# Encoder layer for two sequences: embedding product ahead of the feed-forward part, gate input split early and loaded row by row

## The chip, the cores and the metric

One core of one Trainium2 chip. The metric is the device time of one execution in microseconds (us); lower is better.

## What is computed

One encoder layer with shared weights is applied to two sequences of 1,024 tokens and 1,024 channels, all in float32:

```
x = x + RMSNorm(concat(pool mixer, attention) @ w_out)
x = x + RMSNorm(SwiGLU(RMSNorm(x)))                    D_FF = 2816
e = p @ w_ple_proj                                     p: 1024 x 256
g = sigmoid(x @ w_ple_gate + b_ple_gate)
return x + e * g
```

The change concerns the last three lines. Below, x after the feed-forward residual is called x2, e the embedding product, x2 @ w_ple_gate the gate product.

## The kernel before

The program has three parts.

**Mixer** (0 to 1,008 us). For each sequence: projections, attention, output projection. It leaves the residual x1 in DRAM (`x1_turned`, channels on partitions) and the feed-forward input in `h2_forms`.

**Feed-forward** (1,008 to 2,315 us). The products use a seven-product scheme for 2x2 blocks. `UNITS` lists the work: for each sequence 11 gate/up units, then 8 down units; each unit has 7 steps (`product`, L1158 to L1176). Every float32 operand is held as two float32r halves, a rounded `hi` and the rest `lo`, and every product is three matmuls (hi*hi, hi*lo, lo*hi). ACT rounds (`hi`), DVE subtracts (`lo`). The moving operand lives in `reg`, 7 forms of up to 4 k-tiles; weights pass through `wraw`, `ws` (sums made by POOL) and `ring` (3 slots, one per step). PE, ACT, DVE, POOL and SP each run their own list in program order and meet only at semaphores. SP issues the transfers of the part. During the gate units of sequence 1 the kernel finishes sequence 0: `norm_in` (SP), `norm_step` (ACT, DVE) and an addition on POOL form x2 of sequence 0 row by row (a row is one k-tile, 128 channels x 1,024 tokens, 512 KB) through the three slots of `stg`, and store it in `x2_turned` as plain float32.

**Embedding and gate** (2,315 us to the end). `x2r` holds both halves of the 8 rows of x2 and lies in the memory of `reg`. So the rows of sequence 0 are loaded into `stg` after the last step of the feed-forward part and split there by ACT and DVE. There are 16 tiles m of 128 output channels, 8 for each sequence. PE does per tile: `gate_tile` (48 matmuls of 512 columns), `turn_y` of the tile before (8 transposes), `embed_tile` (12 matmuls). ACT takes the sigmoid, DVE multiplies by e straight out of PSUM and adds x2 (`y_sum`, L2058 to L2070), PE transposes, ACT copies to `yrow`, SP stores. x2 of sequence 1 is made beside the tiles of sequence 0: its 4 MB of f are loaded at once into `fb`, squared in tiles 2 and 3, summed over the channels by PE in the middle of tile 5 (`token_sums`), scaled by DVE in tiles 5 and 6 (L2112), added to x1 by POOL (L928), and split in tile 7. The tokens p are transposed by PE before the first tile of each sequence (`turn_tokens`), and a weight tile of w_ple_proj comes with each tile.

Its tile loop on PE:

```
for m in range(2 * KT):
    gate_tile(m)
    if m % KT == 0:
        turn_tokens(m // KT)
    if m:
        turn_y(m - 1)
    embed_tile(m)
turn_y(2 * KT - 1)
```

## Time and profile before

| | us |
|---|---|
| median of 3 runs (lowest to highest) | 2611.19 (2607.82 to 2617.57) |
| the profiled execution, its device time | 2615.33 |
| its span in the profile | 2613.1 |
| PE busy in the span | 2403.5 (92%) |
| DVE busy | 1678.6 (64%) |
| ACT busy | 1091.4 (42%) |
| POOL busy | 899.3 (34%) |
| DMA engines, mean share of q1 | 42.4% |

PE is TensorE's matmul row, DVE VectorE, ACT ScalarE, POOL GpSimd, SP the queue that issues transfers. The clock column of a stretch is the share of full speed that TensorE was granted: 1.00 is 2.4 GHz, 0.50 is 1.2 GHz. A busy share over the whole span mixes stages; the table by stage in the first group of rows below is what says where PE waits.

### The profile page before, as it was taken

The numbers are of one execution on the slowest core, as the hardware profiler recorded it, in microseconds if no ns is written. First come the engines' busy times: TensorE is split into PE (matmuls) and PEld (weight loads), VectorE is DVE, ScalarE is ACT, GpSimd is POOL, SyncE is SP. The second block draws the span as 40 slices with busy tenths as digits, with TensorE's granted clock in tenths as the row PEclk, the third lists the DMA queues.
The fourth block names the chain that finished last, engine by engine and source line by source line (L and its number), as shares of the span: only waits on it lengthen the run. The fifth ranks groups of instructions, "written<-read, shape, count | busy, mean of one in ns | idle before, by whom it ended". The sixth has DMA issues, their size and how long they took to land.

```text
span 2613.1 us, 32818 instructions
## 1 busy us (share of the span) xinstructions
PE 2403.5 (92%) x11528; PEld 1992.0 (76%) x11528; DVE 1678.6 (64%) x1814; ACT 1091.4 (42%) x1607; POOL 899.3 (34%) x549
## 2 busy tenths in 40 slices
PE   7989999398999992999999999899999999969898
PEld 6878878387788771888888888678788888857677
DVE  6678854266888442777677555788888855554632
ACT  4368854332888442433333322344433332223322
POOL 0024520200445013454444354544455535520300
PEclk9989999699999995999999999999999999989999
DMA  4000022610000346444454876745557687554422
GB/s 140 17 25 25 2 107 81 192 41 14 20 17 1 139 128 207 152 157 153 135 171 164 335 265 215 224 158 199 168 181 249 234 332 267 197 217 150 126 80 71
DMA packets 299889, 376.26 MB, mean 144 GB/s; under 512 B 16464, under 2 KB 213968, under 8 KB 299600
## 3 DMA queue, kind: packets, MB, share of 16 engines
q1 hardware_dynamic: 299152, 372.08, 42.4%
q0 software_dynamic: 576, 2.10, 0.3%
q8 instruction: 93, 1.52, 0.2%
q14 instruction: 68, 0.56, 0.1%
HBM read 249.35 MB, written 124.78 MB: 143 GB/s over the span
## 4 chain that ended last, share of the span: by engine, by line
PE 63%; issue 16%; POOL 8%; DMA 5%; DVE 4%; SPq 2%; ACT 1%; POOLq 1%; DVEq 0%; ACTq 0%
PE ps L1175 42%; PE ps L934 18%; PE ps L937 3%; DMA stg<-h_forms 1%; SPq L506 1%; DMA h_forms<-forms 1%; POOL win_s L785 1%; DMA xb<-x_turned 1%; POOL win_s L793 1%; DVE reg L1859 1%; POOL win_s L794 1%; DVE ring L1850 1%; POOL win_s L780 1%; POOL heads L806 1%; POOL wout_a L829 1%
## 5 line engine op out<-in xcount | busy, mean ns | idle before, releaser
L1175 PE MATMUL ps<-reg,ring 128*128 128x512 f32 x5544 | 1267.2, 391 | 66.7 <-DVEq L1863 47.1
L1175 PEld LDWEIGHTS ps<-reg,ring 128*128 128x128 f32 x5544 | 1044.8, 189 | 288.7 <-issue 47.4
L1271 ACT ACTIVATE ring<-wraw 128x1024 fp32r<-128x1024 f32 (+2 forms) x152 | 143.7, 946 | 413.5 <-PE ps L1175 376.4
L1850 DVE TENSOR_TENSOR ring<-wraw,ring 128x1024 fp32r<-128x1024 f32 (+2 forms) x152 | 228.7, 1505 | 96.5 <-ACT ring L1271 95.7
L934 PE MATMUL ps<-win,ht 128*128 128x512 f32 (+1 forms) x1152 | 234.3, 362 | 40.4 <-DVE win L1706 40.3
L934 PEld LDWEIGHTS ps<-win,ht 128*128 128x128 f32 x1152 | 191.7, 193 | 71.5 <-DVE win L1706 42.8
L934 PE MATMUL ps<-x2r,gsp 128*128 128x512 f32 x768 | 184.6, 400 | 26.6 <-DVE x2r L2076 19.4
L1271 ACT ACTIVATE ring<-ws 128x1024 fp32r<-128x1024 f32 (+2 forms) x114 | 107.9, 947 | 237.8 <-PE ps L1175 226.0
L1790 DVE TENSOR_TENSOR pt<-ps,pt 128x512 fp32r<-128x512 f32 x256 | 172.4, 687 | 48.9 <-ACT pt L1271 46.4
L1850 DVE TENSOR_TENSOR ring<-ws,ring 128x1024 fp32r<-128x1024 f32 (+2 forms) x114 | 175.9, 1543 | 42.5 <-ACT ring L1271 41.4
L934 PEld LDWEIGHTS ps<-x2r,gsp 128*128 128x128 f32 x768 | 148.0, 194 | 60.8 <-issue 16.7
L1271 ACT ACTIVATE pt<-ps 128x512 fp32r<-128x512 f32 x256 | 153.1, 605 | 60.3 <-PE ps L937 56.7
L1760 DVE TENSOR_REDUCE negmax<-ps 128x1 f32<-128x1024 f32 x128 | 155.8, 1217 | 15.1 <-PE ps L934 15.1
L937 PEld LDWEIGHTS ps<-ident,prob 128*128 128x128 f32 x1024 | 126.3, 142 | 46.1 <-DVE pt L1790 15.4
L937 PE MATMUL ps<-ident,prob 128*128 128x128 f32 x1024 | 156.1, 276 | 4.2 <-DVE pt L1790 4.1
L934 PE MATMUL ps<-keys,qs 128*128 128x512 f32 x512 | 154.8, 426 | 1.7 <-ACT prob L1364 1.7
L868 POOL TENSOR_TENSOR ws<-wraw,ws 128x1024 f32<-128x1024 f32 (+2 forms) x38 | 80.1, 2109 | 210.6 <-DMA wraw<-in_w_up 133.2
L934 PE MATMUL ps<-pt,values 128*128 128x512 f32 x512 | 149.4, 415 | 0.0
L1364 ACT ACTIVATE prob<-ps,negmax 128x1024 f32<-128x1024 f32 x128 | 143.2, 1119 | 3.1 <-DVE negmax L1760 3.1
L899 POOL TENSOR_TENSOR acc<-acc,ev 128x1024 f32<-128x1024 f32 x36 | 105.9, 2943 | 103.3 <-DVE ev L1871 103.3
L874 POOL TENSOR_TENSOR ws<-wraw,ws 128x1024 f32<-128x1024 f32 (+2 forms) x38 | 102.5, 2699 | 64.4 <-DVE ring L1850 64.4
L862 POOL TENSOR_TENSOR ws<-wraw 128x1024 f32<-128x1024 f32 (+2 forms) x38 | 101.0, 2658 | 64.1 <-DVE ring L1850 49.6
(199 smaller groups left out, 3064.2 us busy)
## 6 DMA issues: line engine op xcount, KB each, us to landing
reg<-ff_forms SPq DMA_DIRECT2D x42, 1536.0 KB, 10.1
ff_forms<-fhi SPq DMA_DIRECT2D x88, 512.0 KB, 3.2
wraw<-in_w_gate SPq DMA_DIRECT2D x88, 256.0 KB, 4.2
wraw<-in_w_up SPq DMA_DIRECT2D x88, 256.0 KB, 4.6
ff_forms<-ev SPq DMA_DIRECT2D x44, 512.0 KB, 2.9
wraw<-in_w_down SPq DMA_DIRECT2D x48, 384.0 KB, 5.9
stg<-h_forms SPq DMA_DIRECT2D x28, 512.0 KB, 5.6
reg<-ff_forms SPq DMA_DIRECT2D x14, 1024.0 KB, 5.0
```

What stands on the lines that cost most here:

```text
L862: ins = nc.gpsimd.tensor_tensor(s0, raw_block(u, 0, 0), raw_block(u, 1, 0), ALU.subtract)
L868: ins = nc.gpsimd.tensor_tensor(s1, raw_block(u, 1, 1), s0, ALU.subtract)
L874: ins = nc.gpsimd.tensor_tensor(s1, raw_block(u, 0, 1), s1, ALU.subtract)
L899: nc.gpsimd.tensor_tensor(t, t, ev[:, 0], ALU.add).then_inc(S["acc_sum"], 1)
L934: return nc.tensor.matmul(out, lhs, rhs, start=start, stop=stop)
L937: return nc.tensor.transpose(out, src, ident[:])
L1175: last = nc.tensor.matmul(ps[:, 2 * chain + m, :], ring[:, st % 3, a, m, k * P:(k + 1) * P], reg[:, k, i, e, :], start=OPENS[i] and k == 0 ...
L1271: copy = lambda out, src, **k: nc.scalar.activation(out, src, ACT.Copy, **k)
L1364: nc.scalar.activation(prob[:, s % 2, :], pair(2 * (s % 2)), ACT.Exp, bias=negmax[:, s:s + 1], scale=1.0, accum_out=rowsum[:, s:s + 1]).th ...
L1760: V.tensor_reduce(negmax[:, s:s + 1], pair(2 * (s % 2)), AX.X, ALU.max, negate=True)\
L1790: V.tensor_tensor(pt[at][:, 1], ps[:, 4 + half, :].rearrange("p (k n) -> p k n", k=4), f(pt[at][:, 0]), ALU.subtract).then_inc(S["p_split" ...
L1850: V.tensor_tensor(ring_block(u, st, 1), weight_source(u, i), f(ring_block(u, st, 0)), ALU.subtract).then_inc(S["w_split"], 1)
```

## The change

- **Embedding product first.** Before the first feed-forward step SP loads p of both sequences (2 MB) and w_ple_proj (1 MB); PE transposes p (32 transposes) and makes all 16 tiles of e (192 matmuls). ACT copies each tile out of PSUM to `eo`, SP stores it to `e_turned`. The loads of the first weights and of `reg` come behind the loads of p. `y_sum` gets e back from DRAM into `er`.
- **x2 of sequence 0 split early.** Its making starts at step 33 of sequence 1's gate units, one row every 5 steps (`row_at`, five phases), all in fixed slots of `stg`: 0 the row, 1 first x1 and then the `lo` half, 2 the `hi` half. ACT makes `hi`, DVE `lo`; SP stores both to `x2_split` beside the plain row.
- **By rows.** In the last unit each finished step frees one form of `reg`, and SP loads a split row of x2 (1 MB) into it (`x2_in`). PE then runs tiles 0 and 1 together, row by row, with the two halves of each row already there.
- **Own rows for each sequence.** The rows of sequence 1 get memory of their own (other halves of the forms, and `ring`). f of sequence 1 comes through four slots of one row each: squares in tiles 0 and 1, token sums right after tile 2, the scaling, addition and splitting two rows per tile in tiles 4 to 7. Each of these rows is loaded, and stored back for `y_sum`, in its turn.
- `reg` is laid out form by form; loads into it have one piece per partition where they had several. Weights of the gate have three split slots and are asked for three tiles ahead.

```diff
+SQ_AT, SPLIT_AT, TOKENS_AT, ROOT_AT, INV_AT, ROW_AT, ROW_STEPS = 7, (24, 26), (25, 27), 28, 29, 33, 5
+def norm_at(u, i):
+    return NP * u.j + i if u.seq == 1 and not u.down else -1
+def row_at(u, i, phase):
+    n, r = divmod(norm_at(u, i) - ROW_AT - phase, ROW_STEPS)
+    return n if r == 0 and 0 <= n < KT else None
...
+    x2s_d = nc.dram_tensor("x2_split", (P, KT, 2, 2, CH), F32, kind="Internal").ap()
+    e_d = nc.dram_tensor("e_turned", (NSEQ, P, KT, SEQ), F32, kind="Internal").ap()
...
-        reg = sb(s_reg, "reg", [P, KG, NP, 2, CH], F32R)
-        sb(s_reg, "reg_rest", [P, 2 * CH])
+        reg = sb(s_reg, "reg", [P, NP, KG, 2, CH], F32R)
         s_reg.close()
         s_acc = ExitStack()
-        sb(s_acc, "reg_front", [P, 3 * NP * 2 * CH])
-        acc = sb(s_acc, "acc", [P, 8, 2, CH])
...
+        def x2_row(s, k):
+            if s == 0:
+                return reg[:, k, 0:2] if k < NP else reg[:, 1, 2:4]
+            return reg[:, (0, 2, 3, 4, 5, 6)[k], 2:4] if k < 6 else ring[:, k - 6]
...
+                n = row_at(u, i, 0)
+                if n is not None:
+                    if n:
+                        sp.wait_ge(S["x2_out"], 16 * n)
+                        sp.wait_ge(*at_least("x2s_out", 32 * n))
+                    else:
+                        sp.wait_ge(S["stg_free"], PIECES)
+                    sp.dma_start(stg[:, 0], f_d[0, :, n, :]).then_inc(S["stg_in0"], 16)
+                    sp.dma_start(stg[:, 1].rearrange("p (c n) -> p c n", c=2),
+                                 x1t_d[0:2, :, n, :].rearrange("c p n -> p c n")).then_inc(S["stg_in1"], 16)
+                n = row_at(u, i, 3)
+                if n is not None:
+                    sp.wait_ge(S["x2_sum"], n + 1)
+                    sp.dma_start(x2_d[0, :, n, :], stg[:, 0]).then_inc(S["x2_out"], 16)
+                n = row_at(u, i, 4)
+                if n is not None:
+                    sp.wait_ge(S["x2_hi"], n + 1)
+                    sp.dma_start(x2s_d[:, n, :, 0, :], stg[:, 2].rearrange("p (t n) -> p t n", t=2))\
+                        .then_inc(on("x2s_out"), 16)
+                    sp.wait_ge(S["x2_split"], n + 1)
+                    sp.dma_start(x2s_d[:, n, :, 1, :], stg[:, 1].rearrange("p (t n) -> p t n", t=2))\
+                        .then_inc(on("x2s_out"), 16)
+            def gate_in(m):
...
+            def x2_in(k):
+                if k == KT - 1:
+                    sp.wait_ge(S["a_end"], NU - 1)
+                    sp.wait_ge(S["step_done"], NP * (NU - 2))
+                    sp.wait_ge(*at_least("x2s_out", 32 * KT))
+                else:
+                    sp.wait_ge(S["step_done"], NP * (NU - 1) + k + 1)
+                dst = x2_row(0, k).rearrange("p t e n -> p (t e n)").bitcast(F32)
+                sem = on("x2_row") if k == KT - 1 else on(f"op_in{k}")
+                sp.dma_start(dst, x2s_d[:, k].rearrange("p t e n -> p (t e n)")).then_inc(sem, 16)
...
+            sp.dma_start(pwraw[:], w_proj.rearrange("(k p) n -> p k n", p=P)).then_inc(S["p_in"], 16)
+            for s in range(NSEQ):
+                sp.dma_start(ptok[:, s], p[s * NT:(s + 1) * NT].rearrange("t p n -> p t n")).then_inc(S["p_in"], 16)
             for m in range(2):
                 weights_in(UNITS[0], m)
-            for i in range(2):
+            fill_in(0, 0)
+            weights_in(UNITS[1], 0)
+            for i in range(1, 5):
                 fill_in(0, i)
-            weights_in(UNITS[1], 0)
-            for i in range(2, NP):
+                for m in range(4 * i - 4, 4 * i):
+                    e_store(m)
+            for i in range(5, NP):
                 fill_in(0, i)
             for u in UNITS:
                 for i in range(NP):
@@ -662,8 +758,13 @@
...
+                    if u.n == NU - 2 and i == 5:
+                        gate_in(0)
+                        gate_in(1)
+                    if u.n == NU - 1:
+                        x2_in(i - 1 if i else KT - 1)
...
+            def row_in(n):
+                a = 2 * (n % 2)
                 if n >= 2:
-                    sp.wait_ge(S["y_ready"], n - 1)
-                sp.dma_start(xr[:, n % 2], x2_d[0, :, n, :]).then_inc(S[f"xr_in{n % 2}"], 16)
-            def tokens_in(s):
-                if s:
-                    sp.wait_ge(S["pp_turned"], 1)
-                sp.dma_start(ptok[:], p[s * NT:(s + 1) * NT].rearrange("t p n -> p t n")).then_inc(S["p_in"], 16)
-            def x1_in(n):
-                if n >= 2:
-                    sp.wait_ge(S["fx_done"], n - 1)
-                sp.dma_start(xb[:, n % 2].rearrange("p (c n) -> p c n", c=2),
-                             x1t_d[2:4, :, n, :].rearrange("c p n -> p c n")).then_inc(S[f"xb_in{n % 2}"], 16)
+                    sp.wait_ge(*at_least(f"cs_out{n % 2}", 16 * (n // 2)))
...
+                if m + 3 < 2 * KT:
+                    gate_in(m + 3)
+                if m == 0:
+                    for n in range(4, KT):
+                        square_in(n)
+                if m == 2:
+                    row_in(0)
+                    row_in(1)
+                if m and m + 1 < 2 * KT:
+                    e_in(m + 1)
+                    residual_in(m + 1)
+                if 4 <= m < KT:
+                    for n in (2 * (m - 4), 2 * (m - 4) + 1):
+                        row_out(n)
+                        if n + 2 < KT:
+                            row_in(n + 2)
                 if m:
-                    if 2 <= m + 1 < KT:
-                        residual_in(m + 1)
...
+            turn_embed(0)
+            turn_embed(1)
+            for m in range(2 * KT):
+                embed_tile(m)
+            pe.wait_ge(*at_least("e_done", 2 * KT))
...
+                if last:
+                    done.then_inc(S["gate_done"], 1)
...
+            pe.wait_ge(S["g_split"], 2)
+            for j, k in enumerate(ROWS0):
+                if k == KT - 1:
+                    pe.wait_ge(*at_least("x2_row", 16))
+                else:
+                    pe.wait_ge(*at_least(f"op_in{k}", 16 * (2 * len(DPART) + 1)))
+                for m in range(2):
+                    gate_row(m, k, j == 0, j == KT - 1)
+            turn_y(0)
+            for m in range(2, 2 * KT):
+                pe.wait_ge(S["g_split"], m + 1)
+                pe.wait_ge(S["sig_done"], m - 1)
+                for k in range(KT):
+                    if m == KT:
+                        pe.wait_ge(S["x2_split"], KT + k + 1)
+                    gate_row(m, k, k == 0, k == KT - 1)
+                if m == 2:
+                    for t in range(2):
+                        pe.wait_ge(S["sum_split"], 3 + t)
+                        token_sums(t, sumhl, 4 + t)
+                turn_y(m - 1)
             turn_y(2 * KT - 1)
...
+                if -4 <= st < 0:
+                    for m in range(4 * st + 16, 4 * st + 20):
+                        e_tile(m)
+                if inside and u.n == NU - 1 and i in (2, 4):
...
+                    act.wait_ge(S["sum_done"], 4)
+                    root(rnorm[:], pair(4), D).then_inc(S["sum_root"], 1)
...
             def y_sum(m):
-                s, n = divmod(m, KT)
                 t = sig[:, m % 2]
                 dve.wait_ge(S["sig_done"], m + 1)
-                dve.wait_ge(S["proj_done"], m + 1)
-                V.tensor_tensor(t, t, pair(4), ALU.mult).then_inc(S["prod_done"], 1)
+                dve.wait_ge(*at_least(f"er_in{m % 2}", 16 * (m // 2 + 1)))
+                V.tensor_tensor(t, t, er[:, m % 2], ALU.mult).then_inc(S["prod_done"], 1)
                 dve.wait_ge(S["prod_done"], m + 1)
-                if s == 0:
-                    dve.wait_ge(S[f"xr_in{n % 2}"], 16 * (n // 2 + 1))
-                else:
-                    dve.wait_ge(S["fx_done"], n + 1)
-                V.tensor_tensor(t, t, xr[:, n % 2] if s == 0 else fb[:, n], ALU.add).then_inc(S["y_ready"], 1)
-            tile_lo(0)
-            for k in range(KT):
-                use = PLE_USE + k
-                dve.wait_ge(S["x2_hi"], k + 1)
-                V.tensor_tensor(x2r[:, k, 1], stg[:, use % 3, :], f(x2r[:, k, 0]), ALU.subtract)\
-                    .then_inc(S["x2_split"], 1)
...
+                    if m == 1:
+                        dve.wait_ge(S["sq_done0"], KT)
+                        for t in range(2):
+                            dve.wait_ge(S["sum_done"], 2 + t)
+                            sum_halves(t, sumhl)
+                if m in (2, 3):
                     dve.wait_ge(S["sum_root"], 2)
-                    go(V.reciprocal(rnorm[:], rnorm[:]))
-                if m in (5, 6):
-                    for k in range(4 * (m - 5), 4 * (m - 5) + 4):
-                        V.scalar_tensor_tensor(out=fb[:, k], in0=fb[:, k], scalar=gpost2[:, k:k + 1], in1=rnorm[:],
+                    part = rnorm[:, (m - 2) * CH:(m - 1) * CH]
+                    go(V.reciprocal(part, part))
+                if 4 <= m < KT:
+                    for k in (2 * (m - 4), 2 * (m - 4) + 1):
+                        a = 2 * (k % 2)
+                        t = chain_slot(a)
+                        dve.wait_ge(*at_least(f"cs_in{a}", 16 * (2 + k // 2 + 1)))
+                        V.scalar_tensor_tensor(out=t, in0=t, scalar=gpost2[:, k:k + 1],
+                                               in1=rnorm[:].rearrange("p (t n) -> p t n", t=2),
                                                op0=ALU.mult, op1=ALU.mult).then_inc(S["x2_scaled"], 1)
-            y_sum(2 * KT - 1)
+                    for k in (2 * (m - 4), 2 * (m - 4) + 1):
+                        dve.wait_ge(S["x2_hi"], KT + k + 1)
```

PE at the start of the feed-forward part, before. The names: `hrow` and `h` are the last transposes of the mixer, L1175 is `product`.

```order
L937 MATMUL ps<-ident,hrow 128x128 x8
L937 MATMUL ps<-ident,h 128x128 x8
L227 ISA
L952 REGISTER_ALU
L952 COMPARE_AND_BRANCH
L1175 MATMUL ps<-reg,ring 128x512 x3516
```

PE at the same place now (L1294 is `product`):

```order
L1056 MATMUL ps<-ident,hrow 128x128 x8
L1056 MATMUL ps<-ident,h 128x128 x8
L246 ISA
L1071 REGISTER_ALU
L1071 COMPARE_AND_BRANCH
L1056 MATMUL ps<-ident,ptok 128x128 x32
L1053 MATMUL ps<-pturn,psp 128x512 x192
L1294 MATMUL ps<-reg,ring 128x512 x3372
```

The 32 transposes of p and the 192 embedding matmuls stand between the mixer and the first step.

SP in iteration 5 of its tile loop now. `wraw` receives the gate weights of tile 8, `er` and `xr` the embedding and residual rows of tile 6; `x2_turned<-ev` stores a finished row of x2 of sequence 1, and `ev`, `cs3` receive the f and x1 of the row two further on; `y` is the output of tile 4; the last row is the weight tile of iteration 6.

```order
L696 DMA wraw<-in_w_pgate 128x8x128
L788 DMA er<-e_turned 128x1024
L797 DMA xr<-x2_turned 128x1024
L826 DMA x2_turned<-ev 128x1024
L818 DMA ev<-f_turned 128x1024
L820 DMA ev<-x1_turned 128x2x512
L826 DMA x2_turned<-ev 128x1024
L818 DMA ev<-f_turned 128x1024
L820 DMA cs3<-x1_turned 128x2x512
L833 DMA y<-yrow 128x8x128
L696 DMA wraw<-in_w_pgate 128x8x128
```

Each load of f waits until the store of the row before it in the same slot has landed; the weight tile of the next iteration stands behind them all. Before, this loop held no store of x2.

## Rows read from the trace of the kernel before

**Rows 1.** Stages: length, busy time (and instructions) of PE, PEld, DVE, ACT, POOL; clock, DMA share, GB/s.

```profile
1000.00:1038.00 38.00, 7.82 (x24) 5.96 (x24) 12.96 (x8) 9.29 (x9) 7.38 (x4) 0.59 0.78 238
...
2302.00:2345.00 43.00, 24.44 (x95) 18.89 (x94) 20.24 (x18) 10.03 (x11) 7.95 (x3) 0.80 0.61 208
...
2440.00:2500.00 60.00, 43.94 (x193) 35.25 (x192) 40.63 (x28) 19.25 (x22) 23.23 (x8) 0.87 0.41 121
```

**Rows 2.** Timeline of PE at the start of the feed-forward part: start, length, work [idle before].

```profile
1026.09 7.82 PE L1175 MATMUL ps<-reg,ring 128*128 128x512 f32 x24 [47.07 <-DVEq L1863]
1038.26 22.10 PE L1175 MATMUL ps<-reg,ring 128*128 128x512 f32 x84 [4.35 <-DVE ring L1850]
```

**Rows 3.** The first transfer that SP issues for the feed-forward part.

```profile
1008.52 0.39 SPq L542 DMA_DIRECT2D wraw<-in_w_gate  x1
```

**Rows 4.** Two narrow stretches, columns as in group 1.

```profile
1012.00:1024.00 12.00, 0.00 (x0) 0.00 (x0) 5.49 (x2) 4.23 (x4) 7.00 (x3) 0.50 0.81 254
...
2100.00:2120.00 20.00, 20.00 (x90) 16.56 (x89) 15.39 (x13) 9.10 (x12) 11.03 (x6) 1.00 1.04 401
```

**Rows 5.** Timeline of PE from the last feed-forward steps to the end.

```profile
2289.98 24.77 PE L1175 MATMUL ps<-reg,ring 128*128 128x512 f32 x108 [0.24 <-DVE ring L1850]
2329.27 6.78 PE L934 MATMUL ps<-x2r,gsp 128*128 128x512 f32 x18 [14.52 <-DVE x2r L2076]
...
2387.37 1.03 PE L937 MATMUL ps<-ident,sig 128*128 128x128 f32 x8
2388.16 2.98 PE L934 MATMUL ps<-pturn,psp 128*128 128x512 f32 x12
2390.98 11.05 PE L934 MATMUL ps<-x2r,gsp 128*128 128x512 f32 x48
...
2600.62 1.03 PE L937 MATMUL ps<-ident,sig 128*128 128x128 f32 x8
...
2607.03 1.51 PE L937 MATMUL ps<-ident,sig 128*128 128x128 f32 x8 [2.64 <-DVE sig L2070]
```

**Rows 6.** Groups after 2,316 us: line, work, count | busy us, mean ns | idle before.

```profile
L928 POOL TENSOR_TENSOR fb<-fb,xb 128x1024 f32<-128x1024 f32 x8 | 24.9, 3120 | 140.4 <-DVE fb L2112 138.2 <-DMA xb<-x_turned 2.1
L2048 DVE TENSOR_TENSOR gsp<-graw,gsp 128x1024 fp32r<-128x1024 f32 x16 | 19.6, 1224 | 55.7 <-ACT psp L1271 55.5
L2064 DVE TENSOR_TENSOR sig<-sig,ps 128x1024 f32<-128x1024 f32 x16 | 19.5, 1218 | 75.7 <-PE ps L934 75.7
L1626 ACT ACTIVATE sig<-ps,bgate 128x1024 f32<-128x1024 f32 x16 | 17.8, 1113 | 65.7 <-PE ps L934 65.7
...
L1271 ACT ACTIVATE gsp<-graw 128x1024 fp32r<-128x1024 f32 x16 | 16.9, 1056 | 116.1 <-DMA praw<-in_w_proj 116.1
...
L2070 DVE TENSOR_TENSOR sig<-sig,xr 128x1024 f32<-128x1024 f32 x8 | 12.0, 1504 | 0.3
```

**Rows 7.** Transfers after 2,316 us: count, KB each, median us from issue to landing.

```profile
graw<-in_w_pgate SPq DMA_DIRECT2D x16, 512.0 KB, 5.2
y<-yrow SPq DMA_DIRECT2D x16, 512.0 KB, 3.6
```

**Rows 8.** Transfers from 1,880 to 2,300 us, columns as in group 7.

```profile
stg<-f_turned SPq DMA_DIRECT2D x8, 512.0 KB, 5.7
...
x_turned<-stg SPq DMA_DIRECT2D x8, 512.0 KB, 4.3
```

**Rows 9.** Timeline of DVE in gate unit 6 of sequence 1.

```profile
1914.42 1.22 DVE L1938 TENSOR_TENSOR ev<-ev,ps 128x1024 f32<-128x1024 f32 x1 [2.46 <-PE ps L1175]
...
1926.59 1.28 DVE L2003 SCALAR_TENSOR_TENSOR stg<-stg,gpost,rnorm 128x1024 f32<-128x1024 f32 x1 [0.38 <-DMA stg<-f_turned]
...
1928.92 2.62 DVE L1850 TENSOR_TENSOR ring<-wraw,ring 128x1024 fp32r<-128x1024 f32 x1
...
1938.71 3.42 DVE L2003 SCALAR_TENSOR_TENSOR stg<-stg,gpost,rnorm 128x1024 f32<-128x1024 f32 x1
```

**Rows 10.** Timeline of SP's transfers in the same unit.

```profile
1930.29 0.68 SPq L542 DMA_DIRECT2D wraw<-in_w_up  x1
```

537 lines of the change are left out of this document (277 added, 260 removed).

## Prediction, made before the changed kernel had been run

> **What bounds the kernel now.** I read the table by stage first [rows 1]. Over the feed-forward part PE is busy all the time; only three places leave it idle, and they are where a change of order can act: the start of the feed-forward part (7.8 us busy of 38), the start of the gate part (24.4 of 43), and the turn from sequence 0 to sequence 1 (43.9 of 60). Then the timeline of PE at each place. At the first, step 0 runs at 1026.1 after 47 us without work, and steps follow one another without a gap from step 1 on, at 1038.3 [rows 2]; SP asked for the first data at 1008.5 [rows 3] and the DMA engines were 81% busy behind it [rows 4]. At the second, the last step ends at 2314.75 and the first gate matmul starts 14.5 us later; its first 18 take 6.8 us where 48 take 11.05 once it runs steadily [rows 5], and the stretch has a granted clock of 0.80 [rows 1]. From 2314.75 to the end of the span are 298.35 us. That is the tail that the change rebuilds.
>
> **The tail, without new waits.** A tile now costs PE 10.9 us for the gate, 0.8 for the transposes, 2.8 for the embedding (starts 2387.37, 2388.16, 2390.98 [rows 5]). The change leaves 11.7. Tiles 0 and 1 by rows take 2 x 10.9 = 21.8. At the end, transposing the last tile starts at 2607.03 and the span ends 6.1 later; before it stand the sigmoid (1.1), product and sum (1.2 each), with 0.3 for the handing over [rows 6], 3.8 in all, now that no embedding stands there. With the first gate matmul 2.5 us after the last step (an eviction of 1.2 and the landing of the store that it waits for, now behind x2 rows) the tail would be 2.5 + 21.8 + 14 x 11.7 + 0.8 (a last transposing beside the tiles) + 1.1 (token sums) + 3.8 + 6.1 = 200. Will the x2 rows be there? The last unit has seven steps of 12 matmuls, 2.7 us each, so their loads begin at about -19; 8.4 MB until 20 us after the last step want 215 GB/s; 401 GB/s stands in a stretch with large pieces [rows 4]. At that rate a row of 1 MB takes 2.7 us, as long as PE takes for it in two tiles. So I cost the rows at nothing, with the last unit's own matmuls as the cover; if that cover went, PE would wait for the last row, which is asked for only after the last step.
>
> **The tail's new waits.** Three, in order of time after the last step (0).
> 1. PE transposes tile 0 right behind tiles 0 and 1, with nothing between. The gates end at 24.4, tile 0 is summed at 26.8: 2.4 us.
> 2. The token sums are now wanted after tile 2, which ends at 38.5. DVE sums tile 0, splits a weight tile, adds four squares (to 32.4); then SP may load the last of the next four, and only behind it the gate weights of tile 4. These land 5.2 later [rows 7], at 38.1; ACT rounds them (1.06) ahead of its four squares (to 43.4), DVE adds and halves (to 46), PE sums, waits for the second halves, sums (48.3). PE's transposing ends at 49.3 where 40.4 was possible: 9 us, and about 1.6 for a clock that has dropped. The latter is from the 18 matmuls of 6.8 us, which at full clock take 4.1 [rows 5].
> 3. The rows of sequence 1. In tiles 4 to 7 one iteration is a ring of waits over four engines and SP, since the gate weights of the next iteration are asked for behind two stores that must land: DVE scales row a (1.3 [rows 9]), POOL adds x1 (3.1 [rows 6]), SP stores and waits (3.6 [rows 7]), issues two loads (0.9), stores row b and waits (3.6), two loads, the output, the weight tile (1.7 for issuing), which lands after 5.2, ACT rounds (1.06), DVE subtracts (1.22), and only then scales again. That is 21.7, taken as 22, where a tile takes PE 11.7. The first scaling is possible at 78.6 (tile 4 ends at 73.5; sigmoid, sum, weight split 5.1), the fourth at 144.6; row 7 is then split and multiplied after 1.3 + 2 x 3.1 + 1.1 + 1.2 + 1.4, plus 1.4 at a low clock, 12.6. Tile 8 ends at 157, where 120 was possible: 37 us, the largest new wait.
> The seven tiles that follow and the end bring the tail to 157.2 + 1.0 + 7 x 10.9 + 6 x 0.8 + 1.6 + 3.8 + 6.1 = 250.8. Against 298.35 it gives back **47.5 us**.
>
> **The start.** 3.1 MB of p and w_ple_proj stand ahead of the weights. At 280 GB/s, between 254 with small pieces and 401 [rows 4], they are there at about 1,020.5. 32 transposes at half clock (8 take about 1 us at full clock [rows 5], so 16 take 4), rounding and splitting of two tiles (2.1 and 2.4 [rows 6]) let PE begin at 1,029. Sixteen tiles at 2.8 are 45; an eviction (1.1) and 2 us of gaps between ACT's other copies follow: step 0 at 1,077, step 1 at 1,083. Before, step 1 was at 1038.3. **Plus 45.** The embedding was 45 us in the tail, so almost nothing of it is hidden in the gap of 47 us: that gap ends when the memory is free and the data has come, and p has to come first. The price from below is 42 (data at 401 GB/s, no gaps). From above: 22 MB in all (p, weights, `reg`, 8.4 MB of e stored) at 254 GB/s are 87 us, which puts step 1 at 1,096, plus 58. I stay near the lower end, since e is stored in pieces of 4 KB.
>
> **The feed-forward part.** PE is fed by DVE. In gate unit 6 a step's weights are split at 1931.5 and wanted four steps (24 matmuls, 5.45 us at the gate's pace) after 1914.4, at 1936.2 [rows 9]: 4.7 us to spare. Eight more rounding copies on ACT (1.06) and eight subtractions on DVE (1.2) fit. What costs is the order. A row that is due in step 1 is loaded by SP only after the unit's weights, at 1931.0 on the scale of this unit [rows 10]. It lands 5.7 later [rows 8], and DVE, which wants it at 1931.5, holds back the split for the next step; 5.7 less what is spared leaves 1 to 2 us. Of eight rows two stand so. Stores have to land (4.3 [rows 8]) before the next load, at one row per five steps that fits. One us for the two weight splits in the last unit. **Plus 4**, with 0 and 12 as bounds. The layout of `reg` is at nothing: the part's loads were hidden already.
>
> **Sum.** +45 + 4 - 47.5 = +1.5 us on the profiled execution of 2615.33: **2617 us**. That execution is 4.1 above the median of the three, 2611.19, and 2617 is 0.2% above the median. A measurement of this kernel can tell 0.5%, 13 us, from no change.
>
> **Two rules of the Trainium skill.** Scaling takes 1.28 us alone and 3.42 with POOL at work [rows 9]; the product with e read PSUM and took 1.22, the addition of two SBUF rows 1.50 on average [rows 6]. The Trainium skill, SBUF — State Buffer, "Who interferes with whom", says why: a DVE instruction with two SBUF inputs and a GpSimd instruction that reads SBUF exclude each other. It speaks against taking e from SBUF. By that rule the trace agrees, and the product can be held up to one POOL addition; in item 3 it stands beside the ring, so the sum stays. The Trainium skill, DMA: Bandwidth & Descriptors, "Anatomy of one DMA", fits 2.0 us plus size over 436 GB/s, 3.2 us for 512 KB; the weight tile at 5.2 stands against it. An estimate of the ring by that page is 18.9 us, and the sum 9 us lower.
>
> **Rivals.**
> - *A, faster: the ring does not bind.* If SP's waits overlap more than I think (stores landing in under 3 us, weights that come beside them), the rows of sequence 1 stay behind tiles of 11.7 us and the 37 us of item 3 go. For it: after 2,500 the DMA engines of before are lightly loaded, and the ring has no large piece of work. Against: five landings in a row. 2617 - 37 = 2580. Chance 0.20.
> - *B, slower: the start is bound by stores.* ACT may evict a tile only when the store of two tiles earlier has landed, and SP stands between stores waiting for `reg` pieces. With 1.1 + 4.3 + 0.5 us per two tiles PE's 5.6 decides; it turns when a landing takes over 4.5 us, and at the upper bound above it adds 13: 2630. Chance 0.16.
> - *C, slower: DVE starves the ring of weights.* If the loads of x2 rows land over 10 us after issue (split rows, f, x1 and the feed-forward forms in one queue), each of eight rows holds DVE for more than it has to spare, about 5 us: 2617 + 40 = 2657. For it: DVE waits in program order for ACT, ACT for POOL, POOL for DVE. Against: before, the same kind of load gave one wait of 0.38 [rows 9]. Chance 0.12.
> - *Forecast* 0.52, with its own range from 2600 (start 42, ring 20) to 2638 (start 52, ring 25, part 8).
>
> **Numbers.** Faster by over 0.5% is under 2598: A and 0.06 of the forecast, 0.26. Slower is over 2624: B, C less a little, and 0.09 of the forecast, 0.34. Same 0.40. The range takes in A and the forecast and leaves out half of A and most of C: 2580 to 2640.
>
> **What would show it.** Step 1 near 1,083 and 192 embedding matmuls behind one another before it. The first gate matmul within 3 us of the last step. An idle of 7 to 9 us ahead of the token sums. In tile 8 two waits of PE for the split of rows, together over 30 us, and between the scalings of DVE 22 us. I would be wrong if tile 8 starts and ends like its neighbours, if step 1 is past 1,090, or if PE shows waits for `ring` of several us at each row of sequence 0.

## The result, and where the time went

| | before | after |
|---|---|---|
| median (lowest to highest), us | 2613.22 (2607.82 to 2617.57), 4 runs | 2675.84 (2673.46 to 2676.88), 4 runs |
| the profiled execution, device time | 2615.33 | 2676.23 |
| its span | 2613.1 | 2674.4 |

The ratio is 1.0239, with a 95% interval from 1.0217 to 1.0261: the change makes the kernel 2.4% slower. The prediction was 2617 us with a range from 2580 to 2640, and is wrong: neither the time nor the range holds.

The ledger is made from the two traces. For the feed-forward part I compare the moment at which DVE makes the same addition (the one in step 2 of each unit, 38 in all, counted from 0) with the trace of before:

| unit | what the change put ahead of it | later than before, us |
|---|---|---|
| 1 to 21 | the embedding product | 43.8 (42.9 to 43.6 in units 19 to 21) |
| 24 | squares and token sums of sequence 0 | 59.5 |
| 31 | rows of x2 of sequence 0 | 85.0 |
| 37 | loads of x2 rows, gate weights | 86.8 |
| end of the last step | | 2401.92 - 2314.75 = 87.2 |

Unit 24 already holds most of the first row of x2. Counted from unit 23 (57.0) the squares and sums have 13.2 and the rows 28.0, where the table gives 15.7 and 25.5.

From the end of the last step to the end of the span are 2674.4 - 2401.92 = 272.5 us, 25.9 less than the 298.35 of before. The three sections: +43.8 (predicted +45), +43.4 (predicted +4), -25.9 (predicted -47.5); together +61.3, the difference of the spans.

**The start.** Timeline of PE after, against [rows 2] (columns: start, length, work, idle before and its releaser):

```profile
1018.75 6.53 PE L1056 MATMUL ps<-ident,ptok 128*128 128x128 f32 x32 [41.27 <-DMA ptok<-in_p]
1026.84 11.33 PE L1053 MATMUL ps<-pturn,psp 128*128 128x512 f32 x48 [1.56 <-DVE pturn L2162]
1039.80 22.01 PE L1053 MATMUL ps<-pturn,psp 128*128 128x512 f32 x96 [1.62 <-ACT eo L1396]
1062.52 11.16 PE L1053 MATMUL ps<-pturn,psp 128*128 128x512 f32 x48 [0.71 <-ACT eo L1396]
1076.51 33.75 PE L1294 MATMUL ps<-reg,ring 128*128 128x512 f32 x135 [2.82 <-ACT eo L1396]
```

Step 0 is at 1076.5 where 1,077 was predicted, and 192 matmuls stand ahead of it. Small gaps end with ACT's eviction into `eo`; they looked harmless, and runs 5, 10 and 11 show what stands behind them.

**The feed-forward part.** Before, the timeline of PE shows one unbroken piece of work there (1800 matmuls):

```profile
1881.44 408.29 PE L1175 MATMUL ps<-reg,ring 128*128 128x512 f32 x1800 [0.87 <-ACT rnorm L1275]
```

After, the waits from 1,900 to 2,240 us are (engine and line, waited for; total us, times, longest):

```profile
DVE stg L2144 <- DMA stg<-f_turned: 25.8, 5, 8.9
...
PE ps L1294 <- DVE ring L1993: 19.6, 7, 6.2
...
ACT stg L1396 <- POOL stg L1041: 17.1, 6, 9.4
```

L2144 is DVE's scaling of an x2 row, L1993 its split of feed-forward weights. The timeline of DVE shows how the first wait becomes the second: the scaling waits 6.1 us for its load, and two splits of weights that PE needs stand behind it in program order.

```profile
1992.37 1.22 DVE L1993 TENSOR_TENSOR ring<-wraw,ring 128x1024 fp32r<-128x1024 f32 x1
1999.66 1.28 DVE L2144 SCALAR_TENSOR_TENSOR stg<-stg,gpost,rnorm 128x1024 f32<-128x1024 f32 x1 [6.08 <-DMA stg<-f_turned]
2000.86 1.21 DVE L2031 TENSOR_TENSOR ev<-ev,ps 128x1024 f32<-128x1024 f32 x1
2001.99 2.49 DVE L1993 TENSOR_TENSOR ring<-ws,ring 128x1024 fp32r<-128x1024 f32 x1
```

Why loads are late, at another row. In SP's queue the store of the second half goes out at 2079.66, behind a unit's weights, and the next row's load at 2086.70, when that store has landed. DVE scales that row at 2090.70, after the longest of its waits:

```profile
2079.66 0.53 SPq L686 DMA_DIRECT2D x_split<-stg  x1
2086.70 0.33 SPq L673 DMA_DIRECT2D stg<-f_turned  x1
```

```profile
2090.70 1.28 DVE L2144 SCALAR_TENSOR_TENSOR stg<-stg,gpost,rnorm 128x1024 f32<-128x1024 f32 x1 [8.94 <-DMA stg<-f_turned]
```

So the load itself is quick (a median of 4.9 us from 1,900 to 2,240 us, 5.7 in [rows 8]); it is asked for late, behind 16 stores of halves that take 6.2 us each by their median.

Not all of PE's 19.6 us is of this kind. Its longest wait, 6.2 us just before 2202.94, comes after the last row. There DVE waits for a store of the part's own forms (`fhi`), and that store stands in SP's queue behind one load into `reg` that SP needed 6.14 us to issue, where before it took 1.06 and PE did not wait:

```profile
2186.53 6.14 SPq L611 DMA_DIRECT2D reg<-ff_forms  x1
```

```profile
2198.33 1.22 DVE L2113 TENSOR_TENSOR fhi<-ev,fhi 128x1024 fp32r<-128x1024 f32 x1 [8.58 <-DMA ff_forms<-fhi]
```

In the runs below this issue and PE's wait have the same length: 3.96 and 3.99 us in run 1, 3.48 and 3.52 in run 4, 5.54 and 5.58 in run 7, 1.41 and 1.44 in run 8, 6.41 and 6.42 in run 9. Why the issue takes so long is not shown.

The squares earlier in the sequence show the same on ACT. Waits from 1,700 to 1,900 us after:

```profile
ACT stg L1672 <- DMA stg<-f_turned: 26.1, 5, 7.7
...
PE ps L1053 <- DVE sumhl L2118: 8.6, 1, 8.6
```

The second is PE ahead of the token sums; behind that idle time 48 matmuls take 13.22 us at a granted clock of 0.80, where 11.1 is usual at 1.00, so this wait costs more than its own length.

**The tail.** Timeline of PE after, against [rows 5]:

```profile
2407.89 24.79 PE L1053 MATMUL ps<-reg,gsp 128*128 128x512 f32 x96 [5.97 <-DVE ev L2081]
...
2457.30 1.22 PE L1053 MATMUL ps<-sumhl,ones 128*128 128x512 f32 x2 [10.24 <-DVE sumhl L2118]
...
2517.39 1.94 PE L1056 MATMUL ps<-ident,sig 128*128 128x128 f32 x8 [7.35 <-ACT yrow L1396]
2518.98 13.03 PE L1053 MATMUL ps<-reg,gsp 128*128 128x512 f32 x48
2543.55 1.94 PE L1056 MATMUL ps<-ident,sig 128*128 128x128 f32 x8 [11.54 <-ACT yrow L1396]
...
2578.20 4.33 PE L1053 MATMUL ps<-ring,gsp 128*128 128x512 f32 x12 [23.29 <-DVE ring L2255]
```

Five waits of over 5 us, the longest in tile 8 for the last two rows of sequence 1. The timeline of DVE gives the round of waits by its pairs of scalings, 26.2 us apart where 22 was predicted:

```profile
2491.28 2.48 DVE L2250 SCALAR_TENSOR_TENSOR ev<-ev,gpost,rnorm 128x1024 f32<-128x1024 f32 x2
...
2517.51 2.48 DVE L2250 SCALAR_TENSOR_TENSOR ev<-ev,gpost,rnorm 128x1024 f32<-128x1024 f32 x2
...
2543.67 2.48 DVE L2250 SCALAR_TENSOR_TENSOR ev<-ev,gpost,rnorm 128x1024 f32<-128x1024 f32 x2
```

Why 26: one round in the timeline of SP's queue. The store of row b, issued at 2500.38, lets the next load out only at 2506.47, 6.1 us later (3.6 was taken from [rows 7]); the gate weights stand behind all of it, at 2507.82, and ACT can round them at 2515.28, 7.5 us later (5.2 was taken).

```profile
2500.38 0.47 SPq L826 DMA_DIRECT2D x_turned<-ev  x1
2506.47 0.32 SPq L818 DMA_DIRECT2D ev<-f_turned  x1
...
2507.82 0.58 SPq L696 DMA_DIRECT2D wraw<-in_w_pgate  x1
```

### The profile page after: what moved, and what is told of

The parts are those of the page before. It is cut to its first block and busy times, and to the rows that moved or that the text cites. A ratio compares the mean times of both kernels' runs of the same rounds, so it can differ in the third digit from the quotient of the medians.

```text
span 2674.4 us, 32908 instructions
## 1 busy us (share of the span) xinstructions
PE 2414.1 (90%) x11528; PEld 1996.5 (75%) x11528; DVE 1689.1 (63%) x1802; ACT 1101.8 (41%) x1608; POOL 914.8 (34%) x549
## 5 line engine op out<-in xcount | busy, mean ns | idle before, releaser
L1294 PE MATMUL ps<-reg,ring 128*128 128x512 f32 x5544 | 1278.2, 393 | 40.1 <-DVE ring L1993 36.5
L1294 PEld LDWEIGHTS ps<-reg,ring 128*128 128x128 f32 x5544 | 1050.1, 190 | 268.2 <-DVE ring L1993 44.3
L1993 DVE TENSOR_TENSOR ring<-wraw,ring 128x1024 fp32r<-128x1024 f32 (+2 forms) x152 | 229.0, 1509 | 66.4 <-ACT ring L1396 66.2
L1053 PEld LDWEIGHTS ps<-win,ht 128*128 128x128 f32 x1152 | 191.3, 193 | 73.4 <-DVE win L1849 44.5
L1993 DVE TENSOR_TENSOR ring<-ws,ring 128x1024 fp32r<-128x1024 f32 (+2 forms) x114 | 170.9, 1499 | 61.9 <-ACT ring L1396 61.5
L1053 PE MATMUL ps<-reg,gsp 128*128 128x512 f32 x672 | 163.3, 403 | 6.2 <-DVE ev L2081 6.0
L1056 PEld LDWEIGHTS ps<-ident,prob 128*128 128x128 f32 x1024 | 124.6, 141 | 46.6 <-DVE pt L1933 16.6
L1053 PEld LDWEIGHTS ps<-reg,gsp 128*128 128x128 f32 x672 | 130.0, 196 | 34.0 <-issue 6.4
L1017 POOL TENSOR_TENSOR racc<-racc,ev 128x1024 f32<-128x1024 f32 x30 | 88.2, 2942 | 105.2 <-DVE ev L2014 105.2
## 6 DMA issues: line engine op xcount, KB each, us to landing
reg<-ff_forms SPq DMA_DIRECT2D x42, 1536.0 KB, 10.2
```

What stands on the lines that cost most here:

```text
L1017: nc.gpsimd.tensor_tensor(t, t, ev[:, 0], ALU.add).then_inc(S["acc_sum"], 1)
L1053: return nc.tensor.matmul(out, lhs, rhs, start=start, stop=stop)
L1056: return nc.tensor.transpose(out, src, ident[:])
L1294: last = nc.tensor.matmul(ps[:, 2 * chain + m, :], ring[:, st % 3, a, m, k * P:(k + 1) * P], reg[:, i, k, e, :], start=OPENS[i] and k == 0 ...
L1993: V.tensor_tensor(ring_block(u, st, 1), weight_source(u, i), f(ring_block(u, st, 0)), ALU.subtract).then_inc(S["w_split"], 1)
```

## The experiments

The theory after the result (L): the 59 us by which the prediction fell short are waits of an engine for a transfer, met too early in its program order, each in front of work that PE needs. Its rival (W): the change added work to DVE, ACT and POOL, and that work costs time whatever its order. For each kernel I made the table of the ledger again. Its first entry is 39.6 to 44.5 us in the kernels whose start is not edited, by one execution each; so what squares, sums and rows cost is told as a difference of entries of the same trace: unit 24 less the first entry, and unit 31 less unit 24. On that measure the changed kernel has 15.7 for squares and sums (59.5 - 43.8) and 25.5 for the rows (85.0 - 59.5). The kernel before, measured again beside each group of runs, had medians from 2611.65 to 2614.41 us, so differences of under 3 us between two runs say nothing.

### 1. A row scaled one step later

```
-                n = row_at(u, i, 1)          (DVE, scaling)
+                n = row_at(u, i, 2)
```

> The change, but DVE scales a row of x2 of sequence 0 one step later (phase 2 instead of 1). Theory L (engines in program order wait for a transfer that was asked for one step earlier): the 26 us that DVE waits for loads of f in the gate units of sequence 1 fall below 8, PE's waits for weights there shrink with them, and the time falls by 12 to 22 us from 2676, to 2654 to 2664. Theory W (DVE has too much added work, eight subtractions and their contention with POOL): nothing is saved, 2672 to 2680.

Measured: 2663.54 us (2663.02 to 2666.95), ratio 1.0194 (1.0177 to 1.0211), 12.3 us less. The rows cost 69.1 - 55.1 = 14.0 us instead of 25.5. The time is at the upper end of what theory L allowed (2654 to 2664), far from W's 2672 to 2680. DVE's waits for the loads fell from 25.8 to 12.0 us, not below the 8 expected, PE's from 19.6 to 9.2, but ACT's for POOL's addition rose from 17.1 to 28.0:

```profile
ACT stg L1396 <- POOL stg L1041: 28.0, 8, 7.2
...
DVE stg L2144 <- DMA stg<-f_turned: 12.0, 2, 7.6
...
PE ps L1294 <- DVE ring L1993: 9.2, 5, 4.0
```

Order alone, with no work taken away, gave back 11.5 us, nearly half of the rows' cost. Whether the rest sits in the wait that moved to ACT is the question of run 9.

### 2. Squares one step later

```
-                n, odd = divmod(r - SQ_AT - 1, 2)          (ACT, square)
+                n, odd = divmod(r - SQ_AT - 2, 2)
-                n, odd = divmod(r - SQ_AT - 2, 2)          (DVE, sum)
+                n, odd = divmod(r - SQ_AT - 3, 2)
```

> The change, but the squares of f of sequence 0 and their sums come one step later behind the same loads. Theory L: ACT's 26 us of waiting for loads of f before the token sums go, PE's wait of 8.6 us ahead of the first token sum falls below 3, and the time falls by 6 to 14 us, to 2662 to 2670. Theory W: unchanged within 4 us of 2676, since the same work is done.

Measured: 2668.8 us (2666.95 to 2671.76), ratio 1.0212 (1.0195 to 1.0229), 7.0 us less. ACT's waits for f loads from 1,700 to 1,900 us went from 26.1 to 7.7, PE's wait ahead of the token sums from 8.6 to 3.9, and squares and sums cost 49.8 - 40.6 = 9.2 us instead of 15.7. Theory L again, for another engine; PE's wait did not fall below 3 us as expected, and what the remaining 9.2 are was not tried.

### 3. Gate weights asked for ahead of the row stores

```
-                if m + 3 < 2 * KT:
+                if m < 5:
                     gate_in(m + 3)
...
+                if 4 <= m < 2 * KT - 4:
+                    gate_in(m + 4)
                 if 4 <= m < KT:
                     for n in (2 * (m - 4), 2 * (m - 4) + 1):
                         row_out(n)
```

> The change, but in the tile loop from tile 4 on SP asks for gate weights one tile further ahead, in front of the stores and loads of x2 rows. Theory R (a round of waits in which the weight tile stands behind two stores that must land): the distance between DVE's scalings falls from 26 us to 13 to 17, the wait of 23 us in tile 8 falls below 10, and the time falls by 22 to 38 us, to 2638 to 2654. Rival B2 (the tail is bound by what the DMA engines can carry): the distance stays over 22 us and the time within 8 us of 2676.

Measured: 2655.11 us (2651.7 to 2656.9), ratio 1.016 (1.0143 to 1.0177), 20.7 us less, a little short of the 2638 to 2654 expected. The waits of PE for ACT's `yrow` are gone, tile 8 still waits 21.5 us (6.01, 1.64, 12.20, 1.64). First scalings of a pair stand at 2488.38, 2501.28, 2521.89 and 2541.57. The first round is 12.9 us, since its rows are already loaded; the others are 20.6 and 19.7. So the weight tile was one part of the round, 6 us, and not the last: the expected 13 to 17 us between scalings and a wait below 10 in tile 8 did not come. Without the weight tile the landings of rows still make 20, as the waits of DVE for `ev` there show (3.42 and 5.62 us in the round from 2521.89). Rival B2, a tail bound by what the DMA engines carry, asked for over 22 us and is refuted.

### 4. No halves of sequence 0 in the feed-forward part

```
-                    copy(stg[:, 2].bitcast(F32R), stg[:, 0]).then_inc(S["x2_hi"], 1)
...
-                    V.tensor_tensor(stg[:, 1].bitcast(F32R), stg[:, 0], stg[:, 2], ALU.subtract)
...
-                    sp.dma_start(x2s_d[:, n, :, 0, :], stg[:, 2]...)
...
-                    sp.dma_start(x2s_d[:, n, :, 1, :], stg[:, 1]...)
```

This leaves out the split of sequence 0: the last unit loads other data of the same size, and the gate of sequence 0 is not the right one.

> The change without the early split: the rounding copies on ACT, the subtractions on DVE and the stores of both halves of x2 of sequence 0 are left out, and the last unit loads as many bytes of other data in their place, so the gate of sequence 0 is computed from wrong rows. Theory L: the loads of f still come one step before they are wanted, so at least half of the 26 us of DVE's waiting stays; the time falls by 4 to 12 us, to 2664 to 2672. Theory W: the work is gone and with it the loss of the row steps, 20 to 28 us, to 2648 to 2656.

Measured: 2659.22 us (2658.34 and 2660.11, 2 runs), ratio 1.0173 (1.0153 to 1.0194), 16.6 us less: between the two. The rows cost 64.6 - 56.1 = 8.5 us. But DVE still waits 16.5 us for row loads, in four waits, so this run took away work, stores that the next load waits for, and some waits, all at once. It does not separate L from W.

### 5. The start with 2 of 12 embedding matmuls per tile

```
-                for k in range(2):
-                    for t in range(2):
-                        for r, (a, e) in enumerate(((0, 0), (0, 1), (1, 0))):
+                for t in range(2):
+                    mm(ps[:, bank + t, :], psp[:, 0, 0, ...], pturn[:, s, 0, 0, ...], True, True)
```

This leaves out 160 of the 192 matmuls, so e is not the right one; it is copied, stored and loaded all the same.

> The embedding product runs 2 of its 12 matmuls per tile (160 of 192 left out; e is rounded out, stored and loaded all the same, and is wrong). Theory W (the start is paid by the matmuls themselves): the 192 matmuls take 44.5 us in the trace of the changed kernel; with 32 left, a tile costs ACT's eviction of 1.1 us and some gaps, 16 tiles about 22 us in place of 48, so that step 0 comes 20 to 28 us earlier than 1076.5: 2648 to 2656, step 0 near 1052. Theory S (it is paid by memory: stores of e that must land before the next eviction of the same buffer, or the weights behind 3.1 MB of p): two tiles per 1.1 + 4.3 + 0.5 us are 47 us for 16, and step 0 moves by less than 6 us: 2670 to 2677.

Measured: 2677.38 us (2676.39 and 2678.36, 2 runs), ratio 1.0243 (1.0222 to 1.0263): no change. This was the surprise of the study. Timeline of PE in this kernel:

```profile
1039.31 2.40 PE L1053 MATMUL ps<-pturn,psp 128*128 128x512 f32 x4 [4.80 <-ACT eo L1393]
...
1055.21 2.46 PE L1053 MATMUL ps<-pturn,psp 128*128 128x512 f32 x4 [7.68 <-ACT eo L1393]
...
1076.71 23.47 PE L1294 MATMUL ps<-reg,ring 128*128 128x512 f32 x91 [6.53 <-ACT eo L1393]
```

160 matmuls less, and step 0 moves from 1076.51 to 1076.71. PE waits for ACT's evictions, and the waits of ACT name the reason:

```profile
ACT eo L1393 <- DMA e_turned<-eo: 23.0, 10, 5.6
```

That is rival B's mechanism, the eviction that waits for the store of two tiles earlier. In the changed kernel the same line reads 18.6 us in 8 waits, and a store lands after 4.3 us by the median there; the prediction put the turning point at 4.5.

### 6. Runs 1 to 3 together, and the token sums one tile later

The edits of runs 1, 2 and 3, and:

```
-                if m == 2:          (PE: token sums; ACT: root; DVE: halves and reciprocals one later each)
+                if m == 3:
```

> The three moves together (row scaled one step later, squares one step later, gate weights asked for ahead of the row stores), and the token sums and root of sequence 1 one tile later. If they are separate waits, the sums of the single runs add up: 2675.8 - 12.3 - 7.0 - 20.7 = 2635.8, less 8 to 11 for the wait of 10.2 us at the token sums: 2625 to 2628. If the about 4 us by which the start is shorter in each of the single runs belong to all alike and not to the edits, they were counted three times and only one is left: 2633 to 2637. If the waits stand in one another's shadow (rows of sequence 1 start later by the second reciprocal of 3.4 us and the ring of rows still ends at the same time): 2640 to 2646, with an unchanged end of tile 8.

Measured: 2634.07 us (2632.92 to 2636.66), ratio 1.0079 (1.0063 to 1.0096). The number is that of the second case (2633 to 2637), but the two parts of the trace say that it is met for another reason; that the number fits is luck. In the feed-forward part the gains are separate: squares and sums cost 50.0 - 41.1 = 8.9 us, the rows 64.2 - 50.0 = 14.2, as in runs 2 and 1. The tail takes 2631.8 - 2381.2 = 250.6 us, exactly as in run 3 (2649.9 - 2399.1 = 250.8): moving the token sums gave nothing. Their wait of 10.2 us is gone, but one of 7.8 us for `yrow` has come up ahead of turning tile 1, the second reciprocal stands ahead of the rows, and the first scaling is 89.1 us after the last step where it was 89.3. That is the third case's mechanism.

### 7. A third buffer for the rows of sequence 1

```
+        def row_slot(n):
+            return chain_slot(2 * (n % 3)) if n % 3 < 2 else sumsq[:]...
...
-                    sp.wait_ge(*at_least(f"cs_out{n % 2}", 16 * (n // 2)))
-                    sp.wait_ge(S["x2_split"], KT + n - 1)
...
+                    sp.wait_ge(*at_least(f"cs_out{(n - 3) % 2}", 16 * ((n - 3) // 2 + 1)))
+                    sp.wait_ge(S["x2_split"], KT + n - 2)
```

> As the last, and the rows of sequence 1 rotate through three buffers for f and x2 in place of two (the third is sumsq, free once its halves are made), so that a row is loaded behind the store of the row before, and not behind its own buffer's store. If landings make the round (20.0 to 20.3 us between two first scalings with the gate weights asked for ahead), it falls to what DVE, POOL and ACT need in a row, 13 to 15 us: three rounds give back 15 to 20, and what is seen is at most the 21 us that PE still waits in tile 8: 11 to 20 us under the last kernel. If DVE and POOL holding each other up makes it, the round stays over 18 and the gain is under 5.

Measured: 2620.03 us (2613.88 to 2624.69, 10 runs), ratio 1.0028 (1.0018 to 1.0039), 14.0 us under run 6, as expected if landings make the round. Timeline of DVE: pairs of scalings begin at 2468.50, 2481.38, 2495.53 and 2509.66; behind a first round of 12.9 us they are 14.1 us apart, where run 6 has 20.4 and 19.6:

```profile
2495.53 1.28 DVE L2260 SCALAR_TENSOR_TENSOR ev<-ev,gpost,rnorm 128x1024 f32<-128x1024 f32 x1
2497.45 2.92 DVE L2260 SCALAR_TENSOR_TENSOR sumsq<-sumsq,gpost,rnorm 128x1024 f32<-128x1024 f32 x1 [0.64 <-DMA sumsq<-f_turned]
...
2504.99 1.23 DVE L2265 TENSOR_TENSOR reg<-sumsq,reg 128x1024 fp32r<-128x1024 f32 x1 [3.36 <-ACT reg L1406]
...
2509.66 1.28 DVE L2260 SCALAR_TENSOR_TENSOR ev<-ev,gpost,rnorm 128x1024 f32<-128x1024 f32 x1
```

A wait for a load is now 0.6 us. What is left of the round is work: a tile's sum and weight split, scaling, POOL's addition, ACT's rounding, DVE's subtraction. PE waits 12.0 us in tile 8 (2.89, 7.49, 1.65).

### 8. Rows later, and no halves

The edits of runs 1 and 4.

> Row scaled one step later and the early split of sequence 0 left out (data of the same size is loaded in its place): the rows part of the feed-forward part cost 25.5 us in the changed kernel, 14 with the scaling later, 8.5 without the halves. If waits for landings are the whole of it (loads that DVE reaches too early, loads that SP holds back behind stores of the halves), nearly nothing is left with both: 0 to 3 us in that part, 2651 to 2656 in all. If DVE's and POOL's own added work and their holding each other up cost PE time, some 6 to 9 us stay whatever the order: 2657 to 2663.

Measured: 2648.34 us (2644.45 and 2652.23, 2 runs), ratio 1.0132 (1.0108 to 1.0155): both runs lie under the 2657 to 2663 of the second expectation, around the lower edge of the first. The rows cost 57.8 - 58.3, that is nothing (0.2 us if counted from unit 23). Waits from 1,900 to 2,240 us:

```profile
DVE stg L2136 <- DMA stg<-f_turned: 4.8, 2, 3.3
...
PE ps L1289 <- DVE ring L1985: 1.4, 1, 1.4
```

DVE still scales eight rows and POOL still adds them, and PE hardly notices: once their loads have landed, scaling and adding cost nothing. The 25.5 us go in two ways: 11.5 by the order of the scaling alone (run 1), 17.0 by leaving the halves out alone (run 4), all of it by both. Within the 17.0 this does not separate the stores of the halves from ACT's rounding and DVE's subtraction, which were left out with them.

### 9. Halves one step later too

From run 7; rounding (ACT) and subtraction (DVE) at phase 4 instead of 3, their stores moved with them, ahead of the next row's load.

> As e7_third_buffer, and in the feed-forward part ACT rounds and DVE subtracts the halves of an x2 row one step later, so that ACT no longer waits for POOL's addition (27.7 us in 8 waits, up to 7.5, in the trace of e7); the stores of the halves move with them, ahead of the next row's load. Theory W (ACT, held in this wait, rounds the ring of weights late and DVE and PE follow): of the 12.7 us that the rows part still costs, 6 to 10 go: 2610 to 2614. Theory L (only landings count, and the next load now waits for stores that have just been issued): the gain is lost again, the row's load comes 5 us later and DVE waits for it as in the changed kernel: 2618 to 2632.

Measured: 2622.84 us (2614.2 to 2627.29, 8 runs), ratio 1.004 (1.0028 to 1.0053); run 7's interval, 1.0018 to 1.0039, overlaps. By the two traces the rows cost 68.7 - 51.2 = 17.5 us instead of 63.6 - 51.1 = 12.5 (18.2 instead of 15.2 if counted from unit 23). ACT's waits for POOL fell from 27.7 to 6.6 us, and waits for loads rose from 11.0 to 18.9 on DVE and from 9.8 to 21.7 on POOL:

```profile
POOL stg L1051 <- DMA stg<-x_turned: 21.7, 3, 11.0
...
DVE stg L2154 <- DMA stg<-f_turned: 18.9, 4, 8.7
```

The time lies in the range of theory L (2618 to 2632) and outside that of W (2610 to 2614). Taking 21 us of ACT's waiting for POOL away gave nothing back, so what is left of run 1's cost was not that wait. It fits that the two stores of the halves, 0.5 MB each, have to land before the next load into the same buffers; a run with the halves' work kept and their stores taken away was not made.

### 10. Two matmuls per tile, four buffers for e

```
+        def e_slot(m):
+            return eo[:, m % 4] if m % 4 < 2 else fhi[:, m % 4 - 2]...
-                act.wait_ge(*at_least(f"e_out{m % 2}", 16 * (m // 2)))
+                act.wait_ge(*at_least(f"e_out{m % 4}", 16 * (m // 4)))
```

> e5 took 160 of 192 matmuls out of the start and moved step 0 by 0.2 us, with ACT waiting 23.0 us for stores of e in 10 waits. Here the same, with four buffers for e in place of two (the other two in the slots of the feed-forward forms, free until then). If the stores are a second chain, as long as the matmuls, the two together release it: 16 evictions of 1.0 and the copies between are 26 us, step 0 near 1055 to 1062, 2655 to 2663. If the memory itself is full (324, 275, 312, 249, 259 GB/s in the stretches of the start), four buffers only move the wait: step 0 past 1070, 2670 or more.

Measured: 2659.22 us (2658.05 and 2660.38, 2 runs), ratio 1.0183 (1.0162 to 1.0203), 18.2 us under run 5. Step 0 is at 1058.98:

```profile
1058.98 26.35 PE L1298 MATMUL ps<-reg,ring 128*128 128x512 f32 x109 [1.20 <-ACT fhi L1397]
```

Together, runs 5 and 10 say that the start hangs on two chains of nearly the same length, PE's 192 matmuls and ACT's evictions behind their stores. Taking the matmuls away moves nothing, taking both away gives 18 us. What taking the stores' waits alone away does, run 11 shows.

### 11. Four buffers with all matmuls, and the first turned tile copied out earlier

From run 7: `e_slot` as in run 10, and ACT's `y_rows(0)` ahead of the second four squares.

> As e7_third_buffer, with all 12 matmuls per tile, four buffers for e, and ACT copying the first turned tile out ahead of the second four squares. The start is then bound by its matmuls alone, of which 44.5 us are left: PE's waits for ACT there (5.1 us in the changed kernel) shrink by 2 to 4 us. The wait of PE ahead of turning tile 1 (7.6 us in e7) goes, and 1 to 3 us of it come back at the token sums. Together 6 to 10 us under e7: 2610 to 2614, equal to before. If the waits have already been given back inside tile 8 (its rows start by DVE's iterations, which PE's gates set), it is under 3 us: 2617 to 2620.

Measured: 2612.06 us (2609.45 to 2614.25, 10 runs), ratio 1.0002 (0.9993 to 1.0012): equal to before, 8.0 us under run 7, as expected. PE's embedding matmuls have no gap any more:

```profile
1027.72 43.98 PE L1067 MATMUL ps<-pturn,psp 128*128 128x512 f32 x192 [2.40 <-DVE pturn L2178]
1072.81 37.47 PE L1308 MATMUL ps<-reg,ring 128*128 128x512 f32 x164 [1.11 <-ACT fhi L1410]
```

A steadier measure of the start than the ledger's first entry is the time from PE's first transpose of p to step 0: 57.8 us in the changed kernel (1018.75 to 1076.51), 58.0 in run 5, 53.2 here and 41.9 in run 10; the kernels with an unedited start have 56.8 to 58.1. So the stores' chain alone is 4.8 us longer than the matmuls alone, and it is the one that sets the start of the changed kernel.

### 12. Scaling ahead of a tile's sum, late rows of sequence 0

```
             for m in range(2 * KT):          (DVE)
+                if 4 <= m < KT:
+                    ...  wait for the load, scale rows 2 * (m - 4) and 2 * (m - 4) + 1
                 y_sum(m)
...
-                    if u.n == NU - 1:          (SP)
+                    if u.n == NU - 1 and i < 5:
                         x2_in(i - 1 if i else KT - 1)
```

and `y_rows(0)` ahead of rounding a weight tile.

> As e11_four_buffers_early_y, with three orders changed. DVE scales the two rows of an iteration ahead of the sum of a gate tile (3.7 us with the weight split), not behind it: the round of 14.1 us loses these 3.7 and falls under the 11.8 of a tile, so that three rounds give back 2.3 each and the last 3.7: of the 12.0 us that PE waits in tile 8, 9 to 11 go. SP loads rows 4 to 6 of sequence 0 behind the last two stores of f in place of between them: the landing that DVE waits for ahead of the first gate matmul (4.5 us, PE 6.4) falls to what it is alone, PE's wait to 2.5 to 3.5, 3 to 4 us less, unless row 4 then comes late. ACT copies the first turned tile out ahead of rounding a weight tile: of PE's 3.5 us there, 0 to 3 go. Together 12 to 17 us: 2595 to 2600, which would be faster than the kernel before by 0.5%. If POOL and DVE hold each other up in the new order (POOL's two additions of 3.1 us beside DVE's scaling and adding), or the f rows have not landed by then, tile 8 gives back under 4: 2604 to 2609.

Measured: 2604.43 us (2603.11 to 2608.37, 6 runs) beside 2614.41 of before, ratio 0.9966 (0.9954 to 0.9978). It is the first version that is faster than before, by 0.34%, less than the 0.5% that I called safe to tell, though its interval excludes 1. It misses the main expectation of 2595 to 2600 by 4 to 9 us and lies in the second one, 2604 to 2609, which named its two conditions: POOL and DVE holding each other up, or rows of f that have not landed. The wait for the first gate matmul fell from 6.41 to 4.06 us and that ahead of turning tile 1 from 3.52 to nothing, but tile 8 gave back 3 us instead of 9 to 11:

```profile
2503.97 5.49 PE L1068 MATMUL ps<-ring,gsp 128*128 128x512 f32 x12 [9.13 <-DVE ring L2275]
```

The reason is in the timeline of DVE, first scalings of a pair at 2464.43, 2477.31 and 2492.02, with this between them:

```profile
2492.02 1.28 DVE L2246 SCALAR_TENSOR_TENSOR ev<-ev,gpost,rnorm 128x1024 f32<-128x1024 f32 x1 [1.59 <-DMA ev<-f_turned]
2495.95 1.28 DVE L2246 SCALAR_TENSOR_TENSOR ev<-ev,gpost,rnorm 128x1024 f32<-128x1024 f32 x1 [2.64 <-DMA ev<-f_turned]
2497.15 1.22 DVE L2232 TENSOR_TENSOR sig<-sig,er 128x1024 f32<-128x1024 f32 x1
2498.40 3.24 DVE L2235 TENSOR_TENSOR sig<-sig,xr 128x1024 f32<-128x1024 f32 x1
```

Both conditions are met. Waits for loads are back, and DVE's sum beside POOL's addition takes 3.24 us instead of 1.23. The DMA view from 2,455 to 2,510 us shows why loads are late again:

```profile
q1 hardware_dynamic: 13229, 18.93, 98.4%
...
x_turned<-ev SPq DMA_DIRECT2D x6, 512.0 KB, 6.6
ev<-f_turned SPq DMA_DIRECT2D x4, 512.0 KB, 6.2
```

The queue's packets fill 98.4% of the DMA engines' time, against 54.7% from 2,486 to 2,575 us in the changed kernel. I read this as a stretch that is now bound by the memory traffic itself, but that is not shown: it was not tried whether less traffic (x2 of sequence 1 kept on the chip, not stored and read again) would lift that.

The tails, from the end of the last step to the end of the span: 298.35 before, 272.5 in the changed kernel, then 250.8 (run 3), 250.6 (run 6), 236.4 (run 7), 233.1 (run 11) and 226.7 (run 12). The prediction's tail without new waits was 200.

## Why the prediction was wrong

- **The start, +45.** Measured +43.8, and step 0 within 0.5 us of its predicted time. The size is right, the reason is not: the text added up PE's work and gave the stores' chain to rival B as something that begins above 4.5 us of landing. Its own terms say otherwise: 1.1 + 4.3 + 0.5 is 5.9 us per two tiles, more than PE's 5.6, so the turning point was 4.0 and not 4.5. Stores landed after 4.3, and runs 5, 10 and 11 show their chain as the longer one, by 4.8 us. The sum also puts p there at 1,020.5, where 3.1 MB at its 280 GB/s give 1,019.6 (the first transpose started at 1018.75). That the sum of matmuls came so close is luck; it gives a wrong forecast for a change that shortens them, as run 5 shows. Against that, "almost nothing of it is hidden in the gap" held: of 45 us 43.8 came.
- **The feed-forward part, +4.** Measured +43.4, and this term alone takes the result out of the range. The step that failed is the sentence that a late row costs "1 to 2 us" and that "of eight rows two stand so". Two things were wrong with it. It priced only rows: the squares were moved as well, to be reached by ACT one step after their load is asked for, and cost 15.7 us (run 2 takes 6.5 of them away with one step of distance). And for the rows it took the landing of 5.7 us and a slack of 4.7. The landing was right, but a load is asked for only when three stores of the row before have landed, at 6.1 to 6.2 us each by their medians and not the 4.3 of [rows 8], so that DVE waited up to 8.9 us. That stores land before the next load, and that "at one row per five steps that fits", is refuted by SP's queue above, where the load is held until 2086.70. Runs 4, 8 and 9 bear it out: with the halves gone and one step more the rows cost nothing, and with their stores later the cost did not fall. Run 9 is the weakest of the three, since its time does not differ from run 7's beyond the noise. Part of the rows' cost, 5.3 us (79.7 in unit 29, 85.0 in unit 31), comes after the last row, where PE's only wait is the one behind the load into `reg` that SP issues slowly; the prediction has no term for it. Rival C named the symptom, a DVE that holds PE up, and nearly the size (+40), and had a chance of 0.12; its condition, loads of x2 rows that land over 10 us after issue, was not met (4.9 by the median), and 15.7 of the 43.4 us are squares and sums, which it did not name. Its evidence against, one wait of 0.38 us in [rows 9], came from a schedule with other distances, and said nothing on the new ones. Whether eight more copies on ACT and subtractions on DVE fit stays open: no run separates them from their stores.
- **The tail, -47.5.** Measured -25.9. The mechanism was right, three rounds of waits that end in tile 8 with PE waiting for the last rows; sizes failed. In order: the first gate matmul after 6.0 us, not 2.5 (+3.5); tiles 0 and 1 in 24.8 us at a granted clock of 0.88, not 21.8 (+3.0); the token sums (with their two waits and the turning) 15.3 us, not 10.8 (+4.5); each of three rounds 26.2 us, not 22 (+12.7). That is 23.7, nearly the 23.4 by which tile 8 ended later than predicted, 180.6 us after the last step and not 157.2. The landings in a round, 6.1 and 7.5 us, had been taken as the medians 3.6 and 5.2 of [rows 7], from a tail with fewer transfers. The Trainium skill, DMA: Bandwidth & Descriptors, "Anatomy of one DMA — SWDGE (gpsimd) path", gives a fit for transfers issued by GpSimd, 3.2 us for 512 KB as an estimate by it. The transfers here are issued by SP, so the fit is no price for them, which the prediction does not say. From 2,486 to 2,575 us they took 2.6 to 8.1 us by their medians, so the measurement decides, and the estimate of the round by that page (18.9 us) was further off than mine. Its waits ahead of turning, 7.4 and 11.5 us, were not predicted, but they lie inside the rounds: run 3 took them away together with the weight tile's place in the round.
- **Rivals.** A (the round does not bind) is refuted: it binds, and binding cost more than thought. B's mechanism is what sets the start, at its own lower edge, and its 13 us did not come. C has the place and nearly the size, but another mechanism. 2617 + 39.4 (feed-forward) + 21.6 (tail) - 1.2 (start) is 2676.8, against 2676.2 of the profiled execution.
- **What would show it.** The signs were well chosen: step 0, the wait ahead of the token sums (10.2 us, 7 to 9 predicted), the wait in tile 8 (23.3 us, "over 30" predicted, with 18.9 more ahead of turning), "waits for `ring` of several us at each row of sequence 0" as a sign of error. The trace shows seven waits of PE for `ring`, four of them of over 2 us.

## What to carry to other kernels

When work is moved in front of other engines' work, take the distance in time between each load and the instruction that wants it, counting from when the queue can really issue the load, behind the landings that the change puts ahead of it; do so for every moved load, and on every engine that runs its list in order. Where an engine waits for a buffer's store, count the landings in one round and try one more buffer: here a third one was worth 14 us. And before an amount of work is called the price of a stage, ask which second chain is as long or longer; taking the work away by itself shows it in one run.

## What the runs showed of the hardware

- The same 512 KB transfer took, by its median in a stretch, from 2.6 to 8.1 us; under a queue filled to 98.4% the two kinds of transfer shown took 6.2 and 6.6 us.
- DVE's addition of two SBUF tiles took 1.23 us alone and 3.24 beside POOL's addition. The Trainium skill, SBUF — State Buffer, "Who interferes with whom", says that two such instructions exclude each other, and the trace agrees. The prediction had priced this at nothing since it stood beside the round of waits; in run 12, once the round was short, it became part of it.
- An idle time of PE of 8.6 us was followed by 48 matmuls in 13.2 us at a granted clock of 0.80, where 11.1 is usual at 1.00: this wait cost a quarter more than it shows.
- The same load into `reg` took SP between 1.06 and 6.41 us to issue. In the changed kernel and the five runs named beside it PE waited as long as the issue took, within 0.04 us. In the kernel before, with 1.06 us, it did not wait.
- Kernels whose program at the start is the same began the feed-forward part between 39.6 and 44.5 us later than before, by one profiled execution each. Differences of under 5 us there are no finding.
